# One in eight of the expert weight blocks multiplied 128 columns wide in a two-layer decoder step

## What is computed

```python
def swiglu(h, wg, wu, wd):
    return (jax.nn.silu(h @ wg) * (h @ wu)) @ wd

# moe_ffn: tokens are sorted to their two experts, and each expert's rows go through
yb = lax.map(one_block, (xb, blk_e))      # one_block: swiglu(xe, wg[e], wu[e], wd[e])
out = jax.ops.segment_sum(yb * row_gate, row_tok)
```

## Time and profile before

| | us |
|---|---|
| median of 3 runs | 1661.07 (1660.38 to 1661.41) |
| the profiled execution | 1648.65 |
| its span, first to last instruction | 1647.0 |
| TensorE busy multiplying, in the span | 1602.2 (97%) |
| of it the experts' gate and up blocks, line 1305 | 547.8 |
| of it the experts' down blocks, line 1328 | 276.6 |

### The profile page before, as it was taken

How to read it: one execution, slowest core, us unless ns; L and a number is a source line. 1 busy time by engine, 2 the same in 40 slices (tenths; PEclk the granted TensorE clock), 3 DMA queues, 4 the chain that set the end, 5 groups by cost and what they waited for, 6 DMA issues and landing times.

```text
span 1647.0 us, 45323 instructions
## 1 busy us (share of the span) xinstructions
PE 1602.2 (97%) x20702; PEld 1348.4 (82%) x20702; DVE 303.0 (18%) x801; ACT 224.5 (14%) x655; POOL 131.4 (8%) x202
## 2 busy tenths in 40 slices
PE   7999999999999999998999999999999999999998
PEld 5667666666666667766999999999999999999997
DVE  2354630000000245453200001000000010000121
ACT  1244320000000034522100000000000000000100
POOL 3221116000000020111100000000000000000100
PEclk9999999999999899999999999999999999999999
DMA  9923238994333232223799998998989989899892
GB/s 281 238 69 93 71 115 238 361 296 154 119 111 117 75 99 74 71 94 102 253 351 334 330 382 295 346 384 289 375 309 324 394 280 373 306 353 379 303 388 71
DMA packets 192294, 395.23 MB, mean 240 GB/s; under 512 B 9698, under 2 KB 63578, under 8 KB 191952
## 3 DMA queue, kind: packets, MB, share of 16 engines
q1 hardware_dynamic: 176560, 346.31, 59.8%
q0 software_dynamic: 15168, 45.95, 9.1%
q10 hardware_dynamic: 384, 0.13, 0.0%
HBM read 357.23 MB, written 37.09 MB: 239 GB/s over the span
## 4 chain that ended last, share of the span: by engine, by line
PE 96%; DVE 2%; issue 1%; ACT 1%; DMA 0%; SPq 0%; DVEq 0%; ACTq 0%
PE bank L1305 33%; PE bank L1328 17%; PE bank L1217 12%; PE bank L750 6%; PE bank L1234 6%; PE bank L1053 2%; PE bank L733 2%; PE bank L1070 2%; PE bank L718 1%; PE bank L704 1%; PE bank L1026 1%; PE bank L1037 1%; PE bank L721 1%; PE bank L986 1%; PE bank L672 1%
## 5 line engine op out<-in xcount | busy, mean ns | idle before, releaser
L1305 PE MATMUL bank<-arena,ring 128*64 128x112 f32 x11264 | 547.8, 260 | 7.7 <-issue 6.7
L1305 PEld LDWEIGHTS bank<-arena,ring 128*64 128x64 f32 x11264 | 541.3, 137 | 13.8 <-issue 11.7
L1328 PE MATMUL bank<-arena,ring 128*64 128x112 f32 x5632 | 276.6, 260 | 2.1 <-issue 1.4
L1328 PEld LDWEIGHTS bank<-arena,ring 128*64 128x64 f32 x5632 | 272.0, 137 | 5.7 <-issue 4.7
L1217 PE MATMUL bank<-hnT,ring 128*128 128x336 f32 x704 | 200.6, 449 | 1.8 <-DVE hnT L1672 1.8
L1217 PEld LDWEIGHTS bank<-hnT,ring 128*128 128x128 f32 x704 | 134.8, 192 | 67.6 <-issue 3.0
L2117 DVE TENSOR_TENSOR arena<-arena,bank 128x112 f32<-128x112 f32 x176 | 47.8, 272 | 500.9 <-ACT arena L1623 500.9
L750 PE MATMUL bank<-hnT,ring 128*128 128x336 f32 x384 | 119.8, 458 | 0.0
L1623 ACT ACTIVATE arena<-bank 128x112 f32<-128x112 f32 x176 | 46.3, 263 | 509.6 <-PE bank L1305 509.6
L1234 PE MATMUL bank<-arena,ring 128*128 128x336 f32 x352 | 99.6, 446 | 0.0
L750 PEld LDWEIGHTS bank<-hnT,ring 128*128 128x128 f32 x384 | 70.8, 193 | 34.8 <-issue 6.8
(11 more groups left out here) (359 smaller groups left out, 1116.3 us busy)
## 6 DMA issues: line engine op xcount, KB each, us to landing
ring<-in_moe_w_gate SPq DMA_DIRECT2D x88, 1024.0 KB, 9.6
ring<-in_moe_w_up SPq DMA_DIRECT2D x88, 1024.0 KB, 9.4
ring<-in_moe_w_down SPq DMA_DIRECT2D x88, 1024.0 KB, 10.3
ring<-in_w_in SPq DMA_DIRECT2D x18, 1024.0 KB, 7.1
ring<-in_w_gate SPq DMA_DIRECT2D x11, 1024.0 KB, 10.8
ring<-in_w_up SPq DMA_DIRECT2D x11, 1024.0 KB, 12.7
xg_rows<-arena POOLq DMA_DIRECT2D x1, 11200.0 KB, 51.9
y_rows<-arena POOLq DMA_DIRECT2D x1, 10752.0 KB, 94.5
```

Of the source, the lines that this page charges most:

```text
L1305: ins = mm(bank[3 + f % 2][rows, SLOTS * w:SLOTS * w + SLOTS], weights[:, col:col + 64], xg[:, c, :], start=(c == 0), stop=(c == DK - 1))
L1328: ins = mm(bank[5 + c // 4][rows, SLOTS * (c % 4):SLOTS * (c % 4) + SLOTS], weights[:, col:col + 64], hid[:, f, :], start=(f == 0 and c % ...
```

## The change

In each group of eight blocks the last one (`c == DK - 1`) is multiplied as one matmul of 128 columns on all 128 PSUM partitions; the other seven stay two halves of 64. That holds for the gate and up blocks (there `c` is the slice of the model width, the last addition to the accumulator) and for the down blocks (there `c` is the output block). `skip_group_check` is a flag for the program builder and no instruction. Transfers, waits, signals and the other engines' lists stay as they are. Wide blocks: 8 x 22 x 2 = 352 among the gate and up blocks and 8 x 22 = 176 among the down blocks, 528 of 4224 in all.

```diff
@@ -1300,10 +1300,11 @@
-                            for half in range(2):
-                                rows, col = slice(64 * half, 64 * half + 64), 128 * in_group + 64 * half
-                                ins = mm(bank[3 + f % 2][rows, SLOTS * w:SLOTS * w + SLOTS], weights[:, col:col + 64],
-                                         xg[:, c, :], start=(c == 0), stop=(c == DK - 1))
+                            wide_block = 128 if c == DK - 1 else 64
+                            for m0 in range(0, 128, wide_block):
+                                rows, col = slice(m0, m0 + wide_block), 128 * in_group + m0
+                                ins = mm(bank[3 + f % 2][rows, SLOTS * w:SLOTS * w + SLOTS], weights[:, col:col + wide_block],
+                                         xg[:, c, :], start=(c == 0), stop=(c == DK - 1), skip_group_check=True)
                             if c < DK - 1:
                                 pay(ins)
@@ -1323,9 +1324,10 @@
                     for c in range(DK):
-                        for half in range(2):
-                            rows, col = slice(64 * half, 64 * half + 64), 128 * c + 64 * half
-                            ins = mm(bank[5 + c // 4][rows, SLOTS * (c % 4):SLOTS * (c % 4) + SLOTS], weights[:, col:col + 64], hid[:, f, :],
+                        wide_block = 128 if c == DK - 1 else 64
+                        for m0 in range(0, 128, wide_block):
+                            rows, col = slice(m0, m0 + wide_block), 128 * c + m0
+                            ins = mm(bank[5 + c // 4][rows, SLOTS * (c % 4):SLOTS * (c % 4) + SLOTS], weights[:, col:col + wide_block], hid[:, f, :],
                                      start=(f == 0 and c % 4 == 0), stop=(f == FC - 1), skip_group_check=True)
```

## The result

The changed kernel takes 1829.49 us (median of 4 runs, 1826.96 to 1832.18), the kernel before 1660.72 (4 runs, 1653.82 to 1661.41). The ratio is 1.1027, 95% interval 1.1006 to 1.1049: slower by a tenth, or 169 us. The profiled execution took 1832.18 us with a span of 1830.5 us.

What follows compares the result with a forecast made beforehand. The prediction took TensorE's own stream to bound the kernel: 187 us for switches, 0.5 us for nine blocks beside transposes, less 11 us of pauses, +176 us on the median 1661.07, gave 1837 us, range 1800 to 1860.

Steps and rivals of the forecast that it cites:

- What bounds the kernel: TensorE's own stream: a record open for 97% of the span; the experts' stage, 845.5 us long, holds all of the change.
- the wide block by itself: Wide expert block in a run of its own kind: 0.224 us against 0.192, 17 us slower for 528 blocks.
- The switch: Column-width changes around wide expert blocks empty TensorE: 0.36 us added at each of 519, 187 us in all.
- The four terms: Start intervals: into wide 0.20, to second wide record 0.20, back to narrow 0.20, to second narrow pair 0.15 us.
- the lower bound from the transposes: First to second wide record takes 0.15 us, as in transposes ending a pass; 0.31 us added per wide block.
- the second rival: At wide expert blocks the switch drains TensorE but weight loads are fetched ahead: +103 us, 1764 us; chance 0.04.
- What is won back: TensorE's pauses for instructions in the experts' stage mostly vanish: -11 us, bounds 0 and -20.
- The base: Change added to the median before, 1661.07 us, not the profiled 1648.65; the 12 us between them left unexplained.
- No switch: Wide expert blocks among narrow ones run at the wide pace only: +6 us, 1667 us; chance 0.03.
- loads ahead: Weight loads at wide expert blocks are fetched ahead though the array drains: +103 us, 1764 us; chance 0.04.
- faster: Shorter instruction list cures the pauses, wide expert block at a narrow one's price: -11 us, 1650 us; chance 0.02.
- The clock: Drains in the experts' stage lower the clock to 0.50 for a tenth of it: about +100 us, 1940; chance 0.04.

Runs made afterwards that it cites:

- all-wide kernel: Every expert block multiplied 128 columns wide, against the kernel before: 1763.8 us against 1659.66, ratio 1.0635.
- the quarters: Last block of each eight as four matmuls of 32 columns instead of two of 64, against the kernel before: 1781.26 us against 1647.38, ratio 1.0806.
- The repeat: The kernel before run again unaltered, for a profile: 1659.56 us, ratio to the kernel before 1.0000.

## Why the prediction was right

**The time.** 1837 us forecast, 1829.5 measured, in the range of 1800 to 1860.

**What bounds the kernel, and the wide block by itself.** As read. The pace of 0.112 us from rows 4 came back in 8448 records of the all-wide kernel. The wide form is slower even where nothing switches: 1763.8 against 1659.7 us.

**The switch.** The four terms 0.20, 0.20, 0.20 and 0.15 us stand in the profile after to the hundredth, at nearly every one of the 519 wide blocks between narrow ones. The second, 0.20 from a line through 64 and 336 streamed columns, was the one I trusted least; the lower bound from the transposes, 0.15, doesn't hold for ordinary matmuls. Sum forecast 187.5 us, measured 191 from the passes and 189.4 from the pair of runs with half the traffic that shows no clusters. The Trainium skill's rule that a change of tiling mode drains TensorE (TensorEngine Tiling (Array Packing), Key Properties) agrees with every run here; the quarters show it for 64 against 32 columns as well. Its other rule (The Trainium skill, TensorE: Matmul & The Clock Gate, "Step-by-step: what each phase is for"), that weight loads are pulled ahead of matmuls in flight, holds here within one width, where loads start 0.095 us ahead, and not across the change, where the load starts with its multiplication: the second rival, 1764 us, is out.

**What is won back.** This is the mis-sized term: -11 us, and 22 to 23 measured, 2 or 3 beyond its bound of -20. Of these 17 are the evenly spaced pauses. Their count from rows 11 took only the 16 stops in which TensorE has no open record, with 0.16 us for what each hides; shorter ones hide wholly behind records of 0.26 us. By the starts the six middle passes of the profile before lose 13.5 us, 18 for eight. The cause was named rightly, with the spacing, the landings and the half loads as its evidence now; the time that the next packet gains is 1.9 us and not the 1.4 of the text, which left out that the list also got shorter. The other 5 or 6 are clusters that the profile before doesn't show and the forecast had no term for. Together with the 3 us that the switches cost more, this is the 7 or 8 us by which the forecast was too high.

**The base.** I left open why the profiled execution of before lay 12 us under the median. The repeat on another chip, whose profile has the two clusters beside GpSimd's indirect transfers, took the 1660 us, and the first profile has no such clusters. That fits in size: of the two profiles of the kernel before with half loads, the one with clusters falls behind the one without by 6.3 us at the first and by 6.9 us at the last pass, and by 1.5 us in all between them. What decides whether an execution has them isn't known. Adding the change to the median was the right choice, since the changed kernel carries clusters too, though smaller ones (7.7 us in its profile against 13); that a part of them goes had no place in the sum. The difference of the two profiled executions, 183.5 us, isn't the effect of the change: one has the clusters and the other doesn't.

**The rivals.** No switch, loads ahead, faster: all refuted by the timeline of a single wide block. The clock stayed at 1.00 through the stage, although TensorE streams less.

## What to carry to other kernels

For 112 streamed columns a block takes 0.192 us as two halves of 64 columns and 0.224 us as one matmul of 128, in runs of its own kind; a wide block that stands alone among narrow ones costs about 0.36 us more than a narrow one. In a list like this one, keep one width for as long a run as possible, and if both are needed put those of a width side by side: the same instructions in another order were 175 us apart here. Before a form is mixed in, look for the places where the kernel already changes between forms; a few pairs of starts there gave the whole price.

## What the hardware showed that I had not expected

- TensorE's list arrives in packets of 16.4 KB, 256 instructions, and a dense stream of short fp32 matmuls, 6.1 us for each packet, waits at the packet's edge when weight traffic keeps the DMA engines busy for 0.91 of the time; it goes on 1.3 to 1.6 us after the packet has landed. 15 us of 1661 (and of 1647) went when the traffic was halved. After the change a packet lasts 8.2 us, and halving the traffic brought nothing.
- While GpSimd issues six indirect transfers over 7 us, TensorE starts only a few multiplications at a time in some executions, in steps of 0.7 to 1.4 us: 6 to 7 us lost for each group in the kernel before, and 5 us came back when one group was made plain. The fewer multiplications TensorE runs in a us, the less it loses: 13 us for both groups at 20.5, 7 to 9 in the changed kernel at 15.6, none at 8.8.
- The loss at a change of width, 0.1 us over the stream each way, is the same between 128 and 64 and between 64 and 32 columns.
